# A bidirectional SSD scan stage with its TensorE, VectorE and GpSimd programs in another order

## The reference, cut to what matters

```python
a_cs = jnp.cumsum(a, axis=2)
decay = jnp.exp(jnp.where(lower, seg, -jnp.inf))
cb = jnp.einsum('bctgn,bcsgn->bctsg', cc, bc)
y_diag = jnp.einsum('bctsgh,bcsghp->bctghp', cb[..., None] * decay, xdt)
states = jnp.einsum('bcsgn,bcsghp->bcghpn', bc, xdt * decay_end[..., None])
def step(h, inp):
    st, dec = inp
    return h * dec[..., None, None] + st, h
y_off = jnp.einsum('bctgn,bcghpn->bctghp', cc, h_in) * jnp.exp(a_cs)[..., None]
...
y = y_f + _flip_seq(y_r) + xh * d_skip
```

## Time and profile before

| what | value |
|---|---|
| median of 3 runs | 1669.87 us (1667.97 to 1678.6) |
| the profiled execution's own time | 1665.68 us |
| its span | 1663.6 us |
| mean granted clock of TensorE, share of 2.4 GHz | 0.885 |
| busy in the span: PE, DVE, ACT, POOL | 83%, 50%, 40%, 16% |

### The profile page before, as it was taken

How to read it: one execution, slowest core, us unless ns; L and a number is a source line. 1 busy time by engine, 2 the same in 40 slices (tenths; PEclk the granted TensorE clock), 3 DMA queues, 4 the chain that set the end, 5 groups by cost and what they waited for, 6 DMA issues and landing times. The chain is left out here.

```text
span 1663.6 us, 20622 instructions
## 1 busy us (share of the span) xinstructions
PE 1380.5 (83%) x7925; PEld 1200.5 (72%) x7925; DVE 835.2 (50%) x959; ACT 669.0 (40%) x1028; POOL 271.2 (16%) x278
## 2 busy tenths in 40 slices
PE   3999989899989999567678854999984489999980
PEld 1799989799988889335456743998873378888860
DVE  2412432476661111273454549333346089999966
ACT  3433220244441221335445637111022077777753
POOL 0600000000000100245656732000004100000002
PEclk9999999899999999796777756999976799999985
DMA  9972211122113431632333432322534589999945
GB/s 387 406 291 76 77 51 54 58 77 76 65 52 118 138 124 42 202 92 98 114 102 122 164 128 82 116 96 73 200 151 168 203 314 411 406 413 409 415 175 202
DMA packets 61639, 289.09 MB, mean 174 GB/s; under 512 B 8171, under 2 KB 12787, under 8 KB 41206
## 3 DMA queue, kind: packets, MB, share of 16 engines
q1 hardware_dynamic: 48566, 242.18, 38.9%
q0 software_dynamic: 12608, 45.62, 7.0%
q10 hardware_dynamic: 384, 0.16, 0.0%
HBM read 239.51 MB, written 48.43 MB: 173 GB/s over the span
## 5 line engine op out<-in xcount | busy, mean ns | idle before, releaser
L212 PE MATMUL banks<-rounded,rounded 128*128 128x320 f32 (+1 forms) x1168 | 365.5, 313 | 19.9 <-DVE rounded L735 6.6
L213 PE MATMUL banks<-rounded,rounded 128*128 128x320 f32 (+1 forms) x1168 | 363.4, 311 | 0.0
L214 PE MATMUL banks<-rounded,rounded 128*128 128x320 f32 (+1 forms) x1168 | 363.3, 311 | 0.0
L212 PEld LDWEIGHTS banks<-rounded,rounded 128*128 128x128 f32 (+1 forms) x1168 | 220.6, 189 | 21.2 <-issue 13.9
L191 DVE TENSOR_TENSOR rounded<-words,rounded 128x2048 fp32r<-128x2048 f32 x52 | 119.2, 2292 | 226.0 <-ACT rounded L183 223.7
L1877 DVE TENSOR_TENSOR rounded<-words,rounded 128x2048 fp32r<-128x2048 f32 x93 | 212.9, 2290 | 34.1 <-ACT rounded L1868 33.2
L213 PEld LDWEIGHTS banks<-rounded,rounded 128*128 128x128 f32 (+1 forms) x1168 | 220.7, 189 | 0.4
L214 PEld LDWEIGHTS banks<-rounded,rounded 128*128 128x128 f32 (+1 forms) x1168 | 220.5, 189 | 0.3
L1868 ACT ACTIVATE rounded<-words 128x2048 fp32r<-128x2048 f32 x96 | 183.7, 1916 | 48.2 <-PE banks L1995 40.0
L183 ACT ACTIVATE rounded<-words 128x2048 fp32r<-128x2048 f32 x52 | 99.2, 1908 | 138.0 <-PE banks L233 61.2
L1169 ACT ACTIVATE words<-words,words 128x128 f32<-128x128 f32 x320 | 97.8, 388 | 125.5 <-DMA words<-decay_sums 125.5
(11 more groups left out here) (270 smaller groups left out, 2058.4 us busy)
## 6 DMA issues: line engine op xcount, KB each, us to landing
words<-in_units SPq DMA_DIRECT2D x52, 1024.0 KB, 5.0
words<-in_wg SPq DMA_DIRECT2D x32, 1024.0 KB, 7.6
words<-in_wu SPq DMA_DIRECT2D x32, 1024.0 KB, 7.7
words<-in_wd SPq DMA_DIRECT2D x32, 1024.0 KB, 8.5
words<-decay_sums SPq DMA_DIRECT2D x40, 512.0 KB, 3.8
words<-in_w_mod_rest SPq DMA_DIRECT2D x32, 512.0 KB, 5.6
slot_rows<-words POOLq DMA_DIRECT2D x27, 512.0 KB, 24.3
expert_rows<-words POOLq DMA_DIRECT2D x25, 512.0 KB, 9.5
```

The lines of the kernel that those rows point to most:

```text
L212: nc.tensor.matmul(out, lhs[0](k), rhs[0](k), start=(k == 0), stop=False)
L213: nc.tensor.matmul(out, lhs[0](k), rhs[1](k), start=False, stop=False)
L214: last = nc.tensor.matmul(out, lhs[1](k), rhs[0](k), start=False, stop=(k == nk - 1))
```

## The change

On TensorE, the state products of a sub-step (`off`) are issued one sub-step ahead, before the diagonal of the sub-step before them; `state`, `add_parts` and `modulate` are issued behind the diagonal of their sub-step instead of ahead of its state products. The wait on the carried state is given per group instead of per chunk. On VectorE, `take_y(j - 1)` comes ahead of `scale_off(j)`, and `carry(x)` one sub-step later. On POOL, `time_rows` runs two sub-steps ahead in three buffers of XT, right behind the skip part, and `weigh` comes behind it. XT takes the room of SO, which moves onto OF; POOL waits for the stores of the context states before its first skip part.

```diff
--- before.py
+++ after.py
@@ -875,8 +875,8 @@
 
     SLOTS = 4
     E = kit.at(O_HL + 2048, SLOTS, 1024)
-    XT = kit.at(O_HL + 6144, 4, 256)
-    SO = kit.at(O_HL + 7168, 2, 512)
+    XT = kit.at(O_HL + 6144, 6, 256)
+    SO = kit.at(O_TMP + 1792, 2, 512)
     CS = kit.at(O_HL + 5120, T)[0:64]
     XD = kit.at(O_K + 848, 2, 512)
     NCS = kit.at(O_TMP + 3360, 2, NC, 32)
@@ -998,12 +998,12 @@
         def _(pool):
             def time_rows(j):
                 c, g, q = subs[j]
-                if j >= 2:
-                    pool.wait_ge(y_done, j - 1)
+                if j >= 3:
+                    pool.wait_ge(y_done, j - 2)
                 hs = heads4(g, q).start
                 rows = byhead(X[:, c, g * GW + q * 256:g * GW + (q + 1) * 256], 4)
                 dt = DT[:, c, :].rearrange("p (d h) -> p d h", d=2)[:, :, hs:hs + 4]
-                nc.gpsimd.tensor_tensor(XT[:, 2 * (j % 2):2 * (j % 2) + 2, :].rearrange("p d (h n) -> p d h n", h=4),
+                nc.gpsimd.tensor_tensor(XT[:, 2 * (j % 3):2 * (j % 3) + 2, :].rearrange("p d (h n) -> p d h n", h=4),
                                         rows.unsqueeze(1).broadcast_to([P, 2, 4, HD]),
                                         dt.unsqueeze(3).broadcast_to([P, 2, 4, HD]), ALU.mult).then_inc(rows_timed, 1)
 
@@ -1023,18 +1023,20 @@
             time_rows(0)
             time_rows(1)
             pool.wait_ge(states_loaded, 48)
+            for j in range(2):
+                pool.wait_ge(state_stored[j], 16 * NX // 2)
             for j, (c, g, q) in enumerate(subs):
-                if j in x_at:
-                    weigh(pool, nc.gpsimd, x_at[j])
                 if j >= NL + 2:
                     pool.wait_ge(y_steps, j - 1)
                 nc.gpsimd.tensor_tensor(byhead(YK[:, j % 2, :], 4), byhead(X[:, c, g * GW + q * 256:g * GW + (q + 1) * 256], 4),
                                         DSK[:, heads4(g, q)].unsqueeze(2).broadcast_to([P, 4, HD]),
                                         ALU.mult).then_inc(skip_ready, 1)
+                if j + 2 < NS:
+                    time_rows(j + 2)
+                if j in x_at:
+                    weigh(pool, nc.gpsimd, x_at[j])
                 if 1 <= j < NL + 1:
                     finish_y(j - 1)
-                if 1 <= j < NS - 1:
-                    time_rows(j + 1)
 
         @block.tensor
         def _(pe):
@@ -1104,35 +1106,44 @@
                     modulate(early[x])
             pe.wait_ge(exps_done, 4)
             pe.wait_ge(sums_taken, 1)
+            def off(j):
+                c, g, q = subs[j]
+                if not c:
+                    return
+                if j >= 2:
+                    pe.wait_ge(off_scaled, j - 1)
+                elif j == 0:
+                    pe.wait_ge(states_loaded, 48)
+                    pe.wait_ge(state_carried, NF - NX)
+                if c < 4:
+                    pe.wait_ge(state_carried, NF - NX + 4 * (3 - c) + g + 1)
+                ct = CT[:, g, c * P:(c + 1) * P]
+                w4 = slice(g * GW + q * 256, g * GW + (q + 1) * 256)
+                nc.tensor.matmul(ps[:, 5 + j % 2, 0:256], ct, hF[:, c - 1, w4], start=True, stop=True)
+                nc.tensor.matmul(ps[:, 5 + j % 2, 256:512], ct, hb(c)[:, w4], start=True, stop=True).then_inc(off_done, 1)
+
             prepare(0)
+            off(0)
             for j, (c, g, q) in enumerate(subs):
                 if j + 1 < NS:
                     prepare(j + 1)
-                if j in x_at:
-                    state(x_at[j])
-                if j in at_sub:
-                    add_parts(at_sub[j] - 1)
-                    modulate(at_sub[j])
+                    off(j + 1)
                 if j >= 2:
                     pe.wait_ge(y_steps, j - 1)
-                elif j == 0:
-                    pe.wait_ge(states_loaded, 48)
-                    pe.wait_ge(state_carried, NF - NX)
-                if c:
-                    pe.wait_ge(state_carried, NF - NX + 4 * (4 - c))
-                    ct = CT[:, g, c * P:(c + 1) * P]
-                    w4 = slice(g * GW + q * 256, g * GW + (q + 1) * 256)
-                    nc.tensor.matmul(ps[:, 5 + j % 2, 0:256], ct, hF[:, c - 1, w4], start=True, stop=True)
-                    nc.tensor.matmul(ps[:, 5 + j % 2, 256:512], ct, hb(c)[:, w4], start=True, stop=True).then_inc(off_done, 1)
                 pe.wait_ge(rows_timed, j + 1)
                 pe.wait_ge(matrix_ready, j + 1)
                 for h in range(4):
                     o = ps[:, 2 + j % 2, h * HD:(h + 1) * HD]
                     for d in range(2):
                         at = d * 512 + h * P
-                        last = nc.tensor.matmul(o, E[:, j % SLOTS, at:at + P], XT[:, 2 * (j % 2) + d, h * HD:(h + 1) * HD],
+                        last = nc.tensor.matmul(o, E[:, j % SLOTS, at:at + P], XT[:, 2 * (j % 3) + d, h * HD:(h + 1) * HD],
                                                 start=(d == 0), stop=(d == 1))
                 last.then_inc(y_done, 1)
+                if j in x_at:
+                    state(x_at[j])
+                if j in at_sub:
+                    add_parts(at_sub[j] - 1)
+                    modulate(at_sub[j])
             add_parts(NP - 1)
 
         @block.scalar
@@ -1262,14 +1273,14 @@
                 e = E[:, j % SLOTS, :].rearrange("p (d h t) -> p d h t", d=2, h=4)
                 nc.vector.tensor_tensor(e, e, CB[:, (j // 2) % 2, :, :].unsqueeze(2).broadcast_to([P, 2, 4, P]),
                                         ALU.mult).then_inc(matrix_ready, 1)
+                if j:
+                    take_y(j - 1)
                 if c:
                     scale_off(j)
-                if j:
-                    take_y(j - 1)
                 if j in at_sub:
                     take_part(at_sub[j])
-                if j in x_at:
-                    x = x_at[j]
+                if j - 1 in x_at:
+                    x = x_at[j - 1]
                     dve.wait_ge(state_carried, x - NX - 3)
                     carry(x)
             take_y(NS - 1)
```

## The result

| | before | changed |
|---|---|---|
| median | 1669.75 us (4 runs, 1667.97 to 1678.6) | 1647.17 us (4 runs, 1644.4 to 1654.73) |
| ratio to before, 95% interval | | 0.9861 [0.9821, 0.9902] |
| the profiled execution's own time | 1665.68 us | 1654.73 us |
| its span | 1663.6 us | 1653.0 us |
| mean granted clock | 0.885 | 0.889 |

The change makes the kernel 1.4% faster (by the interval 1.0 to 1.8%), 22.6 us in the medians. I had forecast 47.6.

The account below looks back on a forecast made before the run. A chain of TensorE, DVE and POOL was taken to bound sub-steps 0 to 23, POOL chunk 1, TensorE chunk 0. Terms -47.6 - 2.0 + 2.0 = -47.6 us gave 1618.1 us profiled, 1622 us median; range 1604 to 1652.

Parts of the forecast that it names:

- The chain before, and its first cut: Sub-steps 0 to 23: TensorE, DVE and POOL take turns in a chain of 14.86 us a pair; state products come ahead.
- `scale_off(j)` finds them done: Sub-steps 0 to 23: DVE's scaling, which waited 90.7 us for TensorE's state products, finds them done when issued a sub-step ahead.
- The new loop's sum: Sub-steps 0 to 23: links through diagonal, state product, modulation, copy, masks and multiply sum to 10.64 us a pair, 47.6 less.
- So I take 2.4 GHz for chunks 4 to 1: Chunks 4 to 1: TensorE runs at full clock, its longest idle time being 0.4 to 0.6 us, less than in chunk 1.
- The rival of the falling clock: Sub-steps 0 to 23: clock keeps falling once a pair, 13.0 us a pair, 19 us less, 1651 to 1653 us; chance 0.10.
- POOL still bounds: Chunk 1: POOL bounds at 8.75 us a pair, DVE and TensorE's loop being 7.9; 2 us less from the slow last pair.
- Net 2 us more: Chunk 0: TensorE idles 1.9 us behind each of three modulations, 5.7 us, less present waits; ends -10 and +5.
- POOL's order is also in time: Sub-steps 0 to 23: with three buffers, `time_rows` and `weigh` end before the diagonal does at 3.55 us.
- POOL becomes the bound: Rival, sub-steps 0 to 23: POOL's work beside DVE's multiply makes 11.5 us a pair, 37 less, 1632 us; chance 0.13.
- The slower rival, TensorE at half clock throughout: A dense TensorE granted 1.2 GHz needs 15.3 us a pair, 13.3 in chunk 1; 1696 us in all; chance 0.04.

Follow-up runs that it names:

- filling: Changed kernel with unread TensorE products of 256 columns added in sub-steps 2 to 23, three ahead of even diagonals, two ahead of odd: 1640.6 us, ratio 0.9808.
- both edits: Changed kernel with the product of B and C issued a sub-step earlier and the modulation ahead of the diagonal again: 1605.7 us, ratio 0.9563.

## Why the prediction was right or wrong

Between the 47.6 us of the forecast and the 10.6 by which the profiled spans differ lie 37.0: 18.7 in the first stretch (16.7 the clock, 2 the last two pairs), 7.5 in chunk 1, 7.0 in chunk 0, and 3.8 ahead of the loop and behind it.

- **The chain before, and its first cut: right.** "`scale_off(j)` finds them done": the 90.7 us of waits are gone, and the state products ahead alone take the first stretch from 175.3 to 124.8 us (with the clock at 0.96 instead of 0.72).
- **The new loop's sum: right.** 10.64 us a pair was forecast; 10.61 is what a pair at full clock takes, though single links are off by up to 0.5 us and cancel. With the clock held at 1.00 by filling, the stretch is 129.74 us, 45.6 below before against the 47.6 of the forecast; the missing 2 us are the two pairs with the modulation at the odd sub-step, which the sum had at the same 10.64.
- **"So I take 2.4 GHz for chunks 4 to 1": the step that failed most.** The reason given was that TensorE's longest idle time would be "0.4 to 0.6 us", less than in chunk 1. The prediction's own sum says otherwise: a loop of 10.64 us with 8.35 us of TensorE's work in it leaves 2.3 us idle for two waits, twice the 0.4 to 0.6 of each. Measured are 0.94 and 1.43 us, and chunk 1 had 1.32 at most. With these idle times (one of 2.43 us comes only ahead of the last pair's first diagonal) the clock fell in more than half of the pairs, to a mean of 0.82. It cost 16.7 us (146.45 against 129.74) in the first stretch. The rival of the falling clock, given a tenth, had the right place, and its total of 1651 to 1653 us is close to the 1647 and 1650 measured. That is luck: it priced the first stretch at 156 us, 10 us too dear, and the losses in chunks 1 and 0 (the next two steps) hide this.
- **"POOL still bounds" chunk 1: wrong.** I left the masks out of the loop of the odd sub-steps. With the modulation at odd sub-steps the even diagonal, the product of B and C, the masks, the odd multiply, the odd diagonal, the modulation, its copies and the even multiply form one line: at full clock 9.33 us, not 7.9, and 8.75 before. With the product of B and C a sub-step earlier, which takes this link out, a pair takes 7.74 us; so POOL, busy 7.45 of them, did not hold a pair at 8.75 either. With the clock at 0.80 the chunk is 5.5 us longer instead of 2 shorter.
- **"Net 2 us more" in chunk 0: wrong, 9.0.** The idle time behind the modulation was sized rightly (1.64 us, forecast 1.9). The 1.81 us ahead of each odd diagonal were missing, the same link of masks and multiply; issuing the product of B and C earlier took 7.7 us of it away.
- **The start:** the multiply of sub-step 0 comes 5.2 us later. 4.3 of these lie ahead of the loop's own code (the first store of the context states is issued at 694.44 instead of 690.14) and differ from execution to execution (691.56 to 695.58 in the runs here). From that store to the first multiply it is 37.3 us here, 35.5 to 37.5 in all kernels with POOL's new wait for the stores and 36.4 to 36.7 in the three without it: the other 0.9 us are within what executions differ by, and a cost of the new wait of up to 1 us is neither shown nor ruled out.
- **POOL:** "POOL's order is also in time" was right and of no use: undoing it cost nothing, and at full clock the multiply suffers less without it. The rival "POOL becomes the bound" did not come; POOL is busy 8.4 of 10.6 us.
- **Not weighed at all:** that the parts of the change could work against each other. By the medians' ratios: state products ahead 0.9664; state product, carry and POOL's order on top 0.9657, nothing that can be measured in the total, though a pair at full clock goes from 10.35 to 9.7 us; the modulation behind the diagonal 0.9861. That VectorE's copies and masks would stand between the modulation and the next multiply was in my chain; what I did not ask is what the loop would be if the modulation had stayed ahead of the diagonal.

The slower rival, TensorE at half clock throughout, had its place too in single pairs (15.15 us at 0.58, PE full for 15.03), but not as the state of the whole.

Why the clock falls in one pair and not in the next is open: the same instructions with the same idle times ran at either level. What held the clock at 1.00 through the whole stretch was filling.

## What to carry to other kernels

When a chain is cut by issuing something a step ahead, test that cut alone before moving anything else with it: here it gave 3.4%, and an edit that came with it, small products put behind the diagonal with their copies ahead of the next multiply, took 2.0 to 2.6% back, by order and clock together. When an instruction is moved out from between two links of a chain, ask what it was hiding: `prepare`, masks, multiply and diagonal were one line all along, with the modulation as their cover. And a sum made at full clock should be given a second total at the clock that the same code had in the trace, since the filling showed 16.7 us between the two. Check the idle times that such a choice of clock rests on against the sum itself: the loop less the engine's work is what must be idle.

## What the runs showed of the hardware that was not expected

- A fuller TensorE was not a faster one by itself: in chunk 0 it was busy 38.9 of 40.7 us at 1.2 GHz before the change. Adding three products of 256 columns ahead of each diagonal lifted the granted clock there from 0.50 to 0.87, and filling the waits of sub-steps 2 to 23 took it from 0.82 to 1.00. The Trainium skill, page "TensorE: Matmul & The Clock Gate", section "Why this matters for your kernels", ties the clock to TensorE being kept busy. The rows of the filled sub-steps 2 to 23 agree (busy 124.38 of 129.74 us, granted 1.00). Those of chunk 0 do not: before the change TensorE was busy nearly throughout at a granted 0.50, and with both edits it was busy 39.85 of 41.74 us at 0.50 without the added products and 37.30 of 40.59 at 0.87 with them.
- The clock fell within a pair whose idle times were 1.43 us and less (the rows from 754.90); the 2.31 us of idle time before the change had looked like the cause and was not needed.
- A multiply on VectorE takes 1.21 us, and 1.99 us with `time_rows` and `weigh` of POOL beside it (rows at 785.79 and 789.33); `weigh` then takes 2.02 us, where its shortest in this trace is 1.04. The times fit one of the two engines running at a time: `time_rows` starts first and takes its usual 1.04 us, the multiply ends 1.08 us behind it, and `weigh` 0.90 us behind the multiply (alone they take 1.21 and 1.04).
